# First attention in steps of a whole weight tile, both heads' softmax in sequence

## The reference

```
qkv = h @ w_qkv
s = (q . k) * 64**-0.5 + bias[q - k]      # per head, keys of later chunks out
p = softmax(s)
o = p . v
mix = o @ w_o
```

## Time and profile before

| | |
|---|---|
| runs | 976.2 us median of 3 (975.8 to 976.39) |
| profiled execution | 976.58 us, of which the span is 975.3 us |
| TensorE | busy 967.2 us, 99% of the span |
| VectorE | busy 681.0 us, 70% |
| ScalarE | busy 589.4 us, 60% |
| GpSimd | busy 66.3 us, 7% |
| TensorE's granted clock, mean | 0.999 |

### The profile page before, as it was taken

The page is one execution under the profiler, slowest core; times in us unless marked ns, Lnnn a source line. Parts: engine busy times, 40 slices in busy tenths (PEclk is TensorE's granted clock), DMA queues, the critical chain, the costliest instruction groups (busy, mean ns, idle before and its releaser), DMA issues.

```text
span 975.3 us, 13401 instructions
## 1 busy us (share of the span) xinstructions
PE 967.2 (99%) x5146; PEld 825.9 (85%) x5146; DVE 681.0 (70%) x1161; ACT 589.4 (60%) x1042; POOL 66.3 (7%) x80
## 2 busy tenths in 40 slices
PE   8999999999999999999999999999999999999997
PEld 6887788888888898888888888888888888988886
DVE  5777776665668789666665688778767554877564
ACT  6777765544457897655554467547876555684443
POOL 1322110000000242000000000000011000000000
PEclk9999999999999999999999999999999999999999
DMA  9753545655555445555655556455543544335551
GB/s 361 304 190 133 191 173 180 230 175 208 178 194 184 147 168 189 183 190 183 227 177 207 177 200 247 173 177 186 199 167 104 193 152 165 133 130 210 178 189 44
DMA packets 27119, 180.33 MB, mean 185 GB/s; under 512 B 2992, under 2 KB 3888, under 8 KB 6320
## 3 DMA queue, kind: packets, MB, share of 16 engines
q1 hardware_dynamic: 26336, 176.98, 50.9%
q0 software_dynamic: 288, 2.10, 0.6%
q10 hardware_dynamic: 432, 0.39, 0.1%
HBM read 178.41 MB, written 1.05 MB: 184 GB/s over the span
## 4 chain that ended last, share of the span: by engine, by line
PE 99%; DMA 1%; DVE 0%; ACT 0%; SPq 0%; issue 0%; DVEq 0%
PE bank L366 17%; PE bank L293 16%; PE bank L295 16%; PE bank L294 16%; PE bank L372 9%; PE bank L338 9%; PE bank L346 4%; PE bank L308 1%; PE bank L498 1%; PE bank L514 1%; PE bank L619 1%; PE bank L548 1%; DMA front<-in_front 1%; PE bank L309 1%; PE bank L559 1%; PE bank L434 0%
## 5 line engine op out<-in xcount | busy, mean ns | idle before, releaser
L1379 DVE TENSOR_TENSOR lo<-raw,hi 128x1024 fp32r<-128x1024 f32 x318 | 375.9, 1229 | 20.0 <-ACT hi L852 19.9
L852 ACT ACTIVATE hi<-raw 128x1024 fp32r<-128x1024 f32 x318 | 320.2, 1050 | 100.0 <-PE bank L295 98.1
L366 PE MATMUL bank<-X,hi 128*128 128x512 f32 x720 | 177.7, 391 | 0.0
L366 PEld LDWEIGHTS bank<-X,hi 128*128 128x128 f32 x720 | 134.7, 188 | 26.2
L883 ACT ACTIVATE bt<-bank 128x256 f32<-128x256 f32 x135 | 51.3, 382 | 140.1 <-PE bank L372 80.3
L1393 DVE TENSOR_TENSOR zr<-bank,bt 128x256 f32<-128x256 f32 x64 | 27.1, 424 | 108.4 <-ACT bt L883 108.4
L293 PE MATMUL bank<-hi,zh 128*128 128x512 f32 x256 | 100.0, 390 | 0.0
L295 PE MATMUL bank<-hi,zl 128*128 128x512 f32 x256 | 99.8, 390 | 0.0
L294 PE MATMUL bank<-lo,zh 128*128 128x512 f32 x256 | 99.6, 389 | 0.0
L372 PEld LDWEIGHTS bank<-X,lo 128*128 128x128 f32 x720 | 92.3, 191 | 3.5
L372 PE MATMUL bank<-X,lo 128*128 128x256 f32 x720 | 93.4, 283 | 0.0
(11 more groups left out here) (349 smaller groups left out, 1544.6 us busy)
## 6 DMA issues: line engine op xcount, KB each, us to landing
raw<-in_w SPq DMA_DIRECT2D x64, 1024.0 KB, 4.8
raw<-in_rin SPq DMA_DIRECT2D x8, 1024.0 KB, 4.8
raw<-in_wk SPq DMA_DIRECT2D x4, 1024.0 KB, 11.0
raw<-in_wq SPq DMA_DIRECT2D x4, 1024.0 KB, 9.2
raw<-in_wo SPq DMA_DIRECT2D x4, 1024.0 KB, 4.7
raw<-in_mk SPq DMA_DIRECT2D x4, 1024.0 KB, 4.7
raw<-in_mv SPq DMA_DIRECT2D x4, 1024.0 KB, 4.7
raw<-in_rout SPq DMA_DIRECT2D x4, 1024.0 KB, 4.8
```

What stands on the lines that cost most here:

```text
L366: return PE.matmul(bank[banks[j]][:, :], wh[:, c:c + P], x[:, k_, :, :].rearrange("p a b -> p (a b)"), start=k_ == 0, stop=j == 1 and k_ = ...
L852: ACTE.activation(hi[u_ % HIS][:, c], raw[u_ % RAW][:, c], ACT.Copy).then_inc(hi_cut, 1)
L1379: DVE.tensor_tensor(lo[u_ % RAW][:, c], raw[u_ % RAW][:, c], hi[u_ % HIS][:, c].bitcast(F32), ALU.subtract).then_inc(lo_cut, 1)
```

## The change

The loop's order is rewritten on three engines. TensorE does a whole tile at a time (`cols_by_part`, or both calls of `wo`), then values, turning of head 2j-2, scores, turning of head 2j-1; the last goes to bank 2 in steps 1 to 5, bank 5 in steps 6 and 7 and bank 4 in step 8. ScalarE and VectorE do the cut of the next tile's first half at the beginning of a step and that of the second half at its end, and between them the work of both heads one after the other: both joinings, both heads' scores, both softmaxes. No instruction is added or left out.

```diff
@@ TensorE
             if name == "wo":
                 wo(i, (1,))
+                wo(i, (0,))
             else:
-                half(name, i, 0, X2, 0)
+                cols_by_part(name, i, X2, (0, 1))
             if j >= 2:
                 pair_av(j - 2)
+            if j:
+                turn(2 * j - 2, CAUSAL)
             if j < 8:
                 pair_scores(j)
             if j:
-                turn(2 * j - 2, CAUSAL)
-            if j == 8:
-                turn(15, CAUSAL, 4)
-            if name == "wo":
-                wo(i, (0,))
-            else:
-                half(name, i, 1, X2, 1)
-            if 0 < j < 8:
-                turn(2 * j - 1, CAUSAL)
+                turn(2 * j - 1, CAUSAL, 2 if j < 6 else 5 if j < 8 else 4)
@@ ScalarE
+            at_half(name, t, 0)
+            if name != "wo":
+                second(name, 2 * t, scale=0.125 if name == "wq" else 1.0)
+                second(name, 2 * t + 1, scale=0.125 if name == "wq" else 1.0)
+            if j >= 2:
+                a.wait_ge(*full["av", j - 2])
+                ACTE.activation(oh[:, j - 2, :], bank[7][:, 0:S], ACT.Copy).then_inc(o_high, 1)
             for e in range(2):
-                at_half(name, t, e)
-                if name != "wo":
-                    second(name, 2 * t + e, scale=0.125 if name == "wq" else 1.0)
-                if e == 0 and j >= 2:
-                    a.wait_ge(*full["av", j - 2])
-                    ACTE.activation(oh[:, j - 2, :], bank[7][:, 0:S], ACT.Copy).then_inc(o_high, 1)
-                if e == 0 and j:
-                    turned_pair(2 * j - 2)
-                if e and j:
-                    turned_pair(2 * j - 1)
+                if j:
+                    turned_pair(2 * j - 2 + e)
+            for e in range(2):
                 if j < 8:
-                    n = 2 * j + e
-                    a.wait_ge(*free["s", n])
-                    soft(n, TT)
+                    a.wait_ge(*free["s", 2 * j + e])
+                    soft(2 * j + e, TT)
+            at_half(name, t, 1)
+            for e in range(2):
                 if 4 <= j < 8:
                     square("mem", [mem[:, n, :] for n in range(NC)], 2 * (j - 4) + e)
@@ VectorE
-            for e in range(2):
-                at_half(name, t, e)
-                if j < 8:
+            at_half(name, t, 0)
+            if name != "wo":
+                for e in range(2):
+                    joined((k if name == "wk" else q)[:, 2 * t + e, :], name, 2 * t + e, scale=0.125 if name == "wq" else None)
+            if j < 8:
+                for e in range(2):
                     i = 2 * j + e
...
-                if name == "wk":
-                    joined(k[:, 2 * t + e, :], "wk", 2 * t + e)
-                if name == "wq":
-                    joined(q[:, 2 * t + e, :], "wq", 2 * t + e, scale=0.125)
-                if e == 0 and j >= 2:
-                    o_low(j - 2)
-                if e == 1 and j < 8:
-                    split_low("mem", mem[:, j, :], mh, ml, "g_mem_2", j)
-                if j < 8:
-                    soft(i, TT)
+            if j >= 2:
+                o_low(j - 2)
+            if j < 8:
+                split_low("mem", mem[:, j, :], mh, ml, "g_mem_2", j)
+                for e in range(2):
+                    soft(2 * j + e, TT)
+            at_half(name, t, 1)
```

## The result

The changed kernel takes 991.91 us (median of 5 runs, 991.51 to 993.48) against 976.31 before (5 runs, 975.8 to 977.21): 15.6 us more, a ratio of 1.0162 with a 95% interval of 1.0151 to 1.0174. Forecast were 989.1, 12.9 more, in a range of 984.0 to 994.0. The profiled execution took 991.71 with a span of 990.4.

A forecast was written before the change was run, and what follows sets the result against it. TensorE was taken to bound the kernel, busy 967.2 of 975.3 us. Terms -0.3 + 2.7 + 9.1 + 0.6 + 0.8 = 12.9 on a median of 976.2 gave 989.1 us, range 984.0 to 994.0.

The forecast's parts named there:

- seams: TensorE's changes between kinds of work: whole tiles gain 0.04 a step, 0.3 us in all; bounds -1.8 to +1.6.
- waits in steps 1 to 5: TensorE waits for VectorE's late cut in wk and wq tiles: 0.63 in step 1, 0.52 in each other, 2.7 us.
- waits in steps 6 to 8: TensorE waits for VectorE's late cut six matmuls into each wo tile: 3.04 each, 9.1 us in all.
- last values: At the loop's end, the last values wait 0.8 us for copies of turnings 14 and 15, no longer hidden by wo.
- The chain of the cut: From s, TensorE's next-tile start after the small work: copy, both heads' exponentials, reciprocal, cut; TensorE goes on at s + 4.53.
- GpSimd's contention: GpSimd's sums beside the late cut in steps 6 to 8 slow it by 0.2 each, 0.6 us; bounds nothing and 1.6.
- Bank 2: In step 6 wo's first fill needs bank 2 at about s + 0.83, hidden within the wait for the cut.
- Only wo waiting: Rival: the cut ends by s + 4.01, steps 1 to 5 lose nothing, full seam gain; 984.3 us, chance 0.15.
- GpSimd slowing the tail: Rival: reciprocal, scaling and cut stretched by 0.8 in each of eight waits, 6.5 more; 995.6 us, chance 0.06.
- Clock: Rival: TensorE's clock falls in three long wo waits, 18 matmuls at half rate, 4.1 each; 1001.4 us, chance 0.07.
- Faster: Rival: the cut lands before each need and only the seams are left, -1.8; 974.4 us, chance 0.03.
- no change: Rival: the waits come to 2 us or less, which needs wo's three waits gone; chance 0.03.

The follow-up runs named there:

- cut, bank and end mended: Changed kernel with VectorE's second-half cut at the step's beginning, turning 9 in bank 0, half of wo behind step 8's turnings, block order as changed: 976.43 us.
- cut first for wo only: Changed kernel with VectorE's second-half cut made at the step's beginning only in steps 5 to 7, whose next tile is wo: 981.24 us.
- cut first: Changed kernel with one line moved, so VectorE cuts both halves of the next tile's low part at the beginning of every step: 978.7 us.
- filled waits (both kernels): Changed kernel with unread matmuls in wo's three long waits: 8, 12 and 12 gave 990.07 us; 11 each, turning 9 in bank 0, gave 990.13.
- the turnings together: Changed kernel with the scores ahead of both turnings, so that no turning stands between values and scores: 995.39 us.
- the first experiment: Changed kernel with VectorE making both halves of the next tile's low part at the beginning of a step: 978.7 us.

## Why the prediction was right

The way, the place and most of the size came out; the sum was 2.7 short. One of its own signs of being wrong came up as well: the granted clock left 1.00. Term by term, measured by differences between the runs:

| term | forecast | by the medians | by the loop's length | from |
|---|---|---|---|---|
| seams | -0.3 | +0.4 | +0.72 | cut, bank and end mended, over before; the interval of the medians is -0.4 to 1.4 |
| waits in steps 1 to 5 | 2.7 | 2.5 | 2.99 | cut first for wo only, less cut first |
| waits in steps 6 to 8, GpSimd with them | 9.7 | 9.6 to 10.0 | 9.35 | the changed kernel less cut first for wo only (10.9, 10.19), less the clock, and 0.8 for bank 2, whose wait comes out only when the cut is early |
| clock | 0 | 1.7 to 2.1 | 1.64 | filled waits (both kernels), against the changed one |
| last values | 0.8 | 0.9 | 0.75 | cut first less the one with bank and end mended (1.7, 1.55), less 0.8 for the bank |

The loop's column adds up to its 15.45. The forecast was short by 1.0 at the seams and by the whole clock, 1.6. The 0.6 put down for GpSimd, which was not there, made up for a part of that; so much was luck.

- **The chain of the cut** stood as worked out, from the turned copy to TensorE's start, s + 4.51 against s + 4.53 (only the first wait, in step 1, was 0.46 instead of 0.63). That it is the cause is shown from both sides: moved forward in the changed kernel it gives back 13.5 us, moved back in the kernel before it costs 25. One link, the turned copy ahead of the exponentials, was tested by itself and is worth 1.2 to 1.7.
- **GpSimd's contention** was put at 0.6 and is not there, the lower of its bounds. The late cut and the one behind it, in step 6 of the kernel after (VectorE, shortest, median and longest in ns), and the sums on GpSimd:

```profile
L1375 DVE TENSOR_TENSOR lo<-raw,hi x2: 1222/1492/1761, 93.1 to 94.2; 128x1024 fp32r<-128x1024 f32 x2
...
93.73 2.86 POOL L2014 TENSOR_TENSOR sq<-sq,sq 128x256 f32<-128x256 f32 x2 [3.86 <-ACT sq L889]
```

The late cut took 1.22, and so it did in steps 7 and 8, though the sums began half way through it; the one behind it took 1.76, and for that nobody waits. TensorE went on 0.09 later in step 8 than in steps 6 and 7, but not because the cut ended later; the reason stays open.
- **The clock** is the term that was mis-sized. I took nothing, the lower bound, because no row showed a fall after a short wait. It fell behind one of three waits in the profiled execution, at 1.6 us; with the waits filled it stayed at 1.00, and these 1.6 us, by the medians 1.7 to 2.1, went. The Trainium skill (TensorE: Matmul & The Clock Gate, section "HAM oscillation — how this bites in real kernels") had that a TensorE that waits between bursts goes cold. The trace agrees that it falls, but not in every burst, and here not at the start of the burst: six matmuls still ran at full rate. (With the turnings together, in step 6, the burst was slow from its first matmul.) The price of a fall was 1.6 us, not the 4.1 of the rival, which had all 18 matmuls at half rate.
- **The seams** were put at a gain because I priced a turning by the one behind the scores, 0.30; between values and scores it holds 0.48. The sign was wrong, the bound of 0.2 a step held (0.10 in steps 2 to 5, but 0.30 in step 0). Where both turnings stand behind the scores, as I had priced them, the gain comes out: 8.04 a step against 8.09.
- **Bank 2 and the end.** The last values waited 0.87 against 0.8. The bank's wait (s + 0.92) was hidden behind that for the cut, as said, and comes out when the cut is early: in the first experiment TensorE starts wo at 87.22, 0.92 after the block's issue.
- **The rivals.** Only wo waiting: refuted, steps 1 to 5 lose 2.5. GpSimd slowing the tail: refuted. Clock: half right. Faster and no change: refuted.

Left open is what decides whether a given wait lets the clock fall: the changed kernel's five runs had a mean granted clock from 0.995 to 0.997, and no run here tells what set them apart. The length of the wait alone does not: 1.8 us was enough twice, and 3.46 was not, in one and the same execution.

## What to carry to other kernels

Where one engine cuts operands for another and also runs a chain that hangs on that other's results, the cuts go ahead of the chain in its queue: an instruction placed last in a step inherits every wait before it, whatever its own time. Grouping small work to save seams is worth what a row of that very neighbourhood shows, here at most 0.05 us a step, and it takes away the cover that work between two users of a bank, or between a product and its reader, gave for nothing. A wait of some microseconds on TensorE can cost more than itself; after one, the granted clock is to be read.

## What the runs showed of the hardware

- TensorE's clock fell to 0.51 for 3.4 us, 1.5 us after a wait of 3 us had ended, at a price of 1.6 us; in the kernel before with its cut last it fell after two waits of 1.8 us and held after one of 3.46. Filling the waits with matmuls whose result nobody reads held it at 1.00 and gave 1.6 to 2.1 us.
- A cut on VectorE took 1.22 us while sums on GpSimd began half way through it, and the cut behind it, beside these sums, 1.76.
- A turning (three 128 x 128 transposes) holds TensorE for 0.48 between values and scores (tiles of 128 x 64 and 64 x 128), and for 0.30 behind the scores; the two turnings in one go take 0.63.
